# x_hi and x_lo, and raw, w_hi and w_lo, exchange their offsets of 0 and 64 bytes from a multiple of 128 in SBUF

## The reference

```
xn = rmsnorm(h, norm_g)
aq, ak, av, agate, iq, ik, iw, cq, ckv, kr, bgate, mg = split_proj(xn @ w_in)      # 2048 -> 9872
o_a = dsa_attend(aq, ak, av, iq, ik, iw)        # top-k of an indexer's scores
y_a = (o_a * silu(agate)) @ w_o_a
cq = rmsnorm(cq, q_norm_g);  qb = cq @ w_uq
ckv = rmsnorm(ckv, kv_norm_g)
o_b = mla_attend(qb, ckv @ w_uk, ckv @ w_uv, kr)
y_b = (o_b * silu(bgate)) @ w_o_b
g = sigmoid(mg)
h = h + (g[:2048] * y_a + g[2048:] * y_b) @ w_out
y = rmsnorm(h, final_g)
```

## Time and profile before

| | |
|---|---|
| time, median of 3 runs | 821.36 us (820.65 to 822.15) |
| the profiled execution | 821.64 us, its span 819.9 us |
| mean granted clock of TensorE | 0.997 |
| TensorE busy | 806.9 us of the span, 6276 matmuls |
| VectorE, ScalarE, GpSimd busy | 522.7, 358.3, 49.0 us |
| moved by DMA | 138.97 MB, 170 GB/s in the mean |

### The profile page before, as it was taken

One profiled execution on the slowest core, in us unless ns is written; L12 is line 12 of the kernel. 1 busy time (PEld: TensorE's weight loads), 2 busy tenths in 40 slices (PEclk: granted clock), 3 DMA queues, 4 the chain that ended last, 5 costly groups with the idle time before them and its releaser, 6 DMA issues.

```text
span 819.9 us, 15423 instructions
## 1 busy us (share of the span) xinstructions
PE 806.9 (98%) x6276; PEld 779.3 (95%) x6276; DVE 522.7 (64%) x845; ACT 358.3 (44%) x528; POOL 49.0 (6%) x56
## 2 busy tenths in 40 slices
PE   7999999999999999999999999999999999999995
PEld 6999999999999998999999999999999999998885
DVE  6798776899876565456544444556466666745665
ACT  7634444453555583244433434343443333334443
POOL 2231102113100000000000000000000000100001
PEclk9999999999999999999999999999999999999998
DMA  9946455544542475134574555455645446474423
GB/s 322 335 148 209 130 163 184 168 134 150 184 124 96 168 246 189 53 104 145 175 245 153 166 183 164 154 156 164 190 128 182 155 153 204 138 288 152 157 104 115
DMA packets 114549, 138.97 MB, mean 170 GB/s; under 512 B 2832, under 2 KB 99744, under 8 KB 113824
## 3 DMA queue, kind: packets, MB, share of 16 engines
q1 hardware_dynamic: 112400, 130.56, 49.1%
q0 software_dynamic: 1808, 7.53, 2.5%
q10 hardware_dynamic: 288, 0.14, 0.1%
HBM read 134.53 MB, written 3.69 MB: 169 GB/s over the span
## 4 chain that ended last, share of the span: by engine, by line
PE 91%; DVE 4%; ACT 2%; issue 1%; DMA 1%; SPq 0%; ACTq 0%; DVEq 0%
PE ps L574 24%; PE ps L575 23%; PE ps L576 23%; PE ps L933 4%; PE ps L937 3%; PE ps L935 3%; PE ps L954 2%; PE ps L784 1%; DVE w_lo L1325 1%; DMA x_t<-in_x_t 1%; PE ps L690 1%; PE ps L756 1%; PE ps L739 1%; PE ps L745 1%; ACT w_hi L996 1%
## 5 line engine op out<-in xcount | busy, mean ns | idle before, releaser
L996 ACT CAST w_hi<-raw 128x1024 fp32r<-128x1024 f32 (+1 forms) x232 | 239.7, 1040 | 322.5 <-PE ps L576 255.4
L1325 DVE TENSOR_TENSOR w_lo<-raw,w_hi 128x1024 fp32r<-128x1024 f32 (+1 forms) x232 | 280.8, 1229 | 153.7 <-ACT w_hi L996 151.9
L574 PE MATMUL ps<-x_hi,w_hi 128*128 128x288 f32 x1232 | 367.1, 298 | 3.6 <-DVE x_lo L1352 2.9
L575 PE MATMUL ps<-x_lo,w_hi 128*128 128x288 f32 x1232 | 363.4, 295 | 0.0
L576 PE MATMUL ps<-x_hi,w_lo 128*128 128x288 f32 x1232 | 363.1, 295 | 0.0
L574 PEld LDWEIGHTS ps<-x_hi,w_hi 128*128 128x128 f32 x1232 | 231.7, 188 | 8.0 <-issue 6.5
L575 PEld LDWEIGHTS ps<-x_lo,w_hi 128*128 128x128 f32 x1232 | 231.7, 188 | 0.2
L576 PEld LDWEIGHTS ps<-x_hi,w_lo 128*128 128x128 f32 x1232 | 231.5, 188 | 0.0
L576 PE MATMUL ps<-og_hi,w_lo 128*128 128x288 f32 x256 | 75.9, 296 | 0.0
L574 PE MATMUL ps<-og_hi,w_hi 128*128 128x288 f32 x256 | 75.7, 296 | 0.0
L575 PE MATMUL ps<-og_lo,w_hi 128*128 128x288 f32 x256 | 74.6, 292 | 0.0
(11 more groups left out here) (263 smaller groups left out, 761.3 us busy)
## 6 DMA issues: line engine op xcount, KB each, us to landing
raw<-in_w_in SPq DMA_DIRECT2D x75, 1024.0 KB, 5.1
raw<-in_w_out SPq DMA_DIRECT2D x16, 1024.0 KB, 5.4
raw<-in_w_o_a SPq DMA_DIRECT2D x8, 1024.0 KB, 5.3
raw<-in_w_o_b SPq DMA_DIRECT2D x8, 1024.0 KB, 5.3
raw<-in_w_uv SPq DMA_DIRECT2D x4, 1024.0 KB, 5.4
raw<-in_w_uq SPq DMA_DIRECT2D x4, 768.0 KB, 4.5
raw<-in_w_ukt SPq DMA_DIRECT2D x2, 1024.0 KB, 5.9
raw<-in_w_uk SPq DMA_DIRECT2D x2, 1024.0 KB, 5.0
```

Of the source, the lines that this page charges most:

```text
L574: nc.tensor.matmul(out, hi, x_h, start=first, stop=False)
L575: nc.tensor.matmul(out, hi, x_l, start=False, stop=False)
L996: nc.scalar.copy(w_hi[:, step % 2, cols], raw[:, step % RAW, cols]).then_inc(hi_done, pieces_done(q))
L1325: nc.vector.tensor_tensor(w_lo[:, step % 2, cols], raw[:, step % RAW, cols], w_hi[:, step % 2, cols].bitcast(F32), ALU.subtract)\
```

## The change

The order of the tiles in the first row is altered: norm_g_sb goes behind x_lo and small_t behind w_lo.

```
-        (norm_g, x_hi, x_lo, small_t, raw, w_hi, w_lo, ident, ones, rope_tab, lora_g, small_u, x_rstd, o_base) = row(
+        (x_hi, x_lo, norm_g, raw, w_hi, w_lo, small_t, ident, ones, rope_tab, lora_g, small_u, x_rstd, o_base) = row(
             -(-nc.sbuf_base // 64) * 64,
-            ("norm_g_sb", [P, KD]), ("x_hi", [P, KD, NTOK], F32R), ("x_lo", [P, KD, NTOK], F32R), ("small_t", [P, 16]),
+            ("x_hi", [P, KD, NTOK], F32R), ("x_lo", [P, KD, NTOK], F32R), ("norm_g_sb", [P, KD]),
             ("raw", [P, RAW, 2048]),
-            ("w_hi", [P, 2, 2048], F32R), ("w_lo", [P, 2, 2048], F32R), ("ident_sb", [P, P]), ("ones", [P, P]),
+            ("w_hi", [P, 2, 2048], F32R), ("w_lo", [P, 2, 2048], F32R), ("small_t", [P, 16]), ("ident_sb", [P, P]), ("ones", [P, P]),
```

## The result

The kernel after takes 823.17 us (median, 822.85 to 823.53) against 821.12 us before (820.65 to 822.15): the ratio is 1.0024, 95% interval 1.0016 to 1.0033. It is slower by 2.05 us where 808.8 us was forecast. Its profiled execution took 823.07 us, its span 821.3 us, granted clock 0.997.

What follows compares the result with a forecast made beforehand. TensorE's train of matmuls was taken as the bound, priced from start to start. From 821.6 us: -18.7 (x) + 1.6 (VectorE wait) + 4.3 (L933) = -12.8, giving 808.8 us; own range 804 to 815, with rivals 802 to 826.

Steps and rivals of the forecast that it cites:

- Step 1: x matmuls, moving x put on a multiple of 128: each 5.6 ns cheaper, 20.7 us over all 3696.
- Step 2: Gain off the path: 360 early x matmuls lost, 3336 remain (18.7 us); 1.6 us new waiting for w_lo, 160 to 215 us.
- Step 3: L933, L935, L937, 768 matmuls with w moving 64 off: 113.3 becomes 118.9 ns, +4.3 us, all on the path.
- Step 4: og, cq and ckv, 1008 matmuls, stationary now 64 off: 0, bounds -5.6 and +10.5 us.
- theory D: From the follow-up runs, not the prediction: d, moving minus stationary address mod 128, sets price; 64 cheap, 0 dear.
- Step 5: ScalarE's casts and VectorE's splits on raw, w_hi and w_lo 64 off: cost nothing.
- Step 6: DMA loads into raw: 0; at 0.2 us per load, hidden except some 0.2 to 1 us in the first 20 us.
- B: Slower: 288-column matmuls pay for length, x keeps 132.1 ns, only the L933 group loses; +4.3, 825.7 us; chance 0.23.
- A: No effect: offsets of 64 do not matter to TensorE, 132 ns is the price of 288 columns; 821.4 us; chance 0.19.
- C: Faster: the stationary operand counts, og, cq and ckv gain 5.6 us more, L933 still loses; 803.2 us; chance 0.10.

Runs made afterwards that it cites:

- the exchange without its side effects: Against before: x at 0, w 64 off as in after, raw kept at 0, everything behind w_lo moved up 64 bytes; 821.06 us against 820.99, ratio 1.0003.
- the first cut kernel: Layout of before, merge-gate and gate loops streaming only the first 256, 272, 240 and 224 of 288 columns; timed once, 799.01 us.

## Why the prediction was wrong

**Step 1, the price of x, failed, and with it the sum.** It read 5.6 ns between ckv and L933 as the price of the moving operand's own offset from a multiple of 128. The 5.6 ns are real, but they belong to the pair: ckv lies at d = 96 from its weights, L933's w at d = 64 from x, and ckv's rows alternate mod 256 while those of w do not. x already lay at d = 64 before, so there was nothing to gain, and the exchange kept it there. Gain: 0 instead of 18.7 us. All rows needed to see a second reading were on the table of addresses; the prediction listed both operands' offsets for each train and then varied only one. With x alone moved to a multiple of 128, x became 1.1 ns dearer, not 5.6 cheaper. The prediction also carried 5.6 ns from 256 to 288 columns, where the table's whole spread over d is 1.1 ns; the 13.5 ns between ckv and og could not show that the price is the same at both lengths, since both lie at 96.

**Step 2** (3336 on the path, a new wait of 1.6 us near 206 us) was never put to the test, since TensorE ran no faster. The sums above use its 3336, but can't tell it from all 3696, which would add 0.4 us. The wait for w_lo that did grow, 0.6 us more, is no sure sign of raw's place: with raw at 0 it was 0.9 us in the exchange without its side effects and 2.2 us in the first cut kernel.

**Step 3** (L933 +4.3 us) failed for the same reason: 113.3 ns stayed, because d stayed at 64. Its size was right for d = 0, where the runs give 119.1.

**Step 4** (og, cq, ckv 0) was off by 1.0 us: d went from 96 to 32, and 132.3 became 133.4 ns. It took its 0 from qa's 131.8 ns, and that reading is not safe. By theory D qa, whose two operands both lie 96 off (d = 0), should take 133.3 ns. The 12 matmuls of the earlier trace rows stand at the start of a train and are irregular: their 11 distances give 131.9 before and 133.5 after, though no operand of theirs moved. qa's next 11 matmuls, before:

```profile
323.10 0.29 PE L575 MATMUL ps<-ckv_lo,qa_hi 128*128 128x288 f32 x1
...
324.43 0.29 PE L576 MATMUL ps<-ckv_hi,qa_lo 128*128 128x288 f32 x1
```

They take 1.33 / 10 = 133 ns, more than og's 132.3, so qa does not speak against D; 11 starts can't settle 1.1 ns, 160 can. The bounds of -5.6 and +10.5 held it.

**Step 5** (casts and splits 0) was right: the 512-column split took 693 ns after the earlier trace rows, the cast 604 [612].

**Step 6** (loads 0, at most 0.2 to 1 us at the start) named the mechanism and its place, but took the lower end; raw alone cost 1.0 us. From 420 us on the longer loads were hidden, TensorE being busy for all of 240 us; that they were not at the start is the reading given above.

**The rivals.** That 823.2 us lies inside the range of 802 to 826 is luck: the range reached up there for B, by a loss at L933 that did not come. A named the outcome for x and L933 but not the reason: offsets do matter, by up to 0.9% of the time, when x moves alone. The rule of the Trainium skill, "SBUF — State Buffer", section "Specifications (TRN2)", on lines of 16 bytes does not account for the runs: all offsets tried are multiples of 16, and yet x at 0 and 32 gave 828.3 and 828.7 us, at 64 821 and at 96 823. B had the right sign, 2.5 us too high. C fell: with w moved to 64, og did not gain but lost.

## What to carry to other kernels

Where a train of matmuls is the bound, read the addresses of both operands of a matmul together: a shift of one of them alone cost up to 0.9% here, and a shift of both that kept their distance mod 128 nothing that shows (+0.1 us, -0.5 to +1.0). Before trusting a price read from two trains, list everything in which they differ (here the pair's distance, the length and the step from row to row) and measure over 100 starts or more. A tile that DMAs write is best put on a multiple of 256 bytes where its loads are not hidden: here raw off one cost 1.0 us (0.2 to 1.7).

## What the runs showed of the hardware

- The pitch of these fp32r matmuls depends on the distance of the two operands mod 128: 133.3 ns at d = 0 and 132.2 at d = 64 for 288 columns, 119.0 and 113.6 for 256 columns with steady rows. It is a repeating rhythm: three matmuls at 134.5, 129 and 133 ns for og at d = 96 before, 131.7, 132.5 and 132.5 at d = 64 once og was moved there, at the same mean. The distance does not always fix it: 133.3 and 134.3 ns with x at 32, 117.8 and 118.9 for 256 columns of x at d = 0.
- Length is not paid column by column: 224, 240, 256 and 272 columns of x took 111.6, 111.8, 116.6 and 125.2 ns at d = 64, and 256 columns took 113.4 once only even rows moved, which keep their place mod 256.
- Not settled: why the distance counts (that both operands are read from the same memory at once is only argued), and why 288 columns reach no less than 132.2 ns in any arrangement tried, where 256 reach 113.3.
